# Scores with the keys on the partitions: attention of a hybrid decoder layer rewritten

## The reference

```python
# D: one shared key and value head, keys chosen by an index score
index = sum_h iw[q,h] * relu(iq[q,h] . ik[s]) * idx_scale      # causal, 8 index heads
sel = top_k(index, 256)
o_dsa = softmax(q.k[sel] * scale) . v[sel]
# nsa: two groups of four heads, three branches, gates by sigmoid
p_c = softmax(q.kc * scale)            # C: 127 compressed keys
imp = p_c summed over the 4 heads, onto 32 blocks of 64 keys by overlap
sel = top_k(imp with forced blocks, 8)
o_s = softmax over the keys of the selected blocks (S)
o_w = softmax over the last 512 keys (W)
out = g0*o_c + g1*o_s + g2*o_w
```

## Time and profile before

| | |
|---|---|
| three timed runs | 4241.75 us median (4239.13 to 4256.56) |
| profiled execution's own time, its span | 4248.7 us |
| busy in the span: PE, DVE, ACT, POOL | 3741.8, 2353.1, 1908.3, 564.5 us |
| attention, in the profile | 569 to 2475 us |
| busy there: PE, DVE, ACT, POOL | 1614, 1567, 1357, 369 us |
| granted PE clock there | 0.87 |

### The profile page before, as it was taken

How to read it: one execution, slowest core, us unless ns; L and a number is a source line. 1 busy time by engine, 2 the same in 40 slices (tenths; PEclk the granted TensorE clock), 3 DMA queues, 4 the chain that set the end, 5 groups by cost and what they waited for, 6 DMA issues and landing times. The chain is left out here.

```text
span 4248.7 us, 62435 instructions
## 1 busy us (share of the span) xinstructions
PE 3741.8 (88%) x20968; PEld 3259.9 (77%) x20968; DVE 2353.1 (55%) x6486; ACT 1908.3 (45%) x3882; POOL 564.5 (13%) x659
## 2 busy tenths in 40 slices
PE   6999677788889877977978969699999999999997
PEld 5999566677778777867877958588788878878885
DVE  4222148889888888888887534333343334324323
ACT  2000147777778766866866633232223223222221
POOL 0000022222221122122021113200020002002001
PEclk9999757888889888988988989899999999999998
DMA  4222231100000000000000035433333433333342
GB/s 144 63 63 69 63 90 34 45 27 27 27 27 27 17 11 27 17 11 21 11 11 16 4 117 158 148 94 97 126 100 98 143 104 94 111 131 99 99 133 75
DMA packets 296102, 295.35 MB, mean 70 GB/s; under 512 B 20272, under 2 KB 237616, under 8 KB 293680
## 3 DMA queue, kind: packets, MB, share of 16 engines
q1 hardware_dynamic: 294368, 290.10, 22.4%
q10 hardware_dynamic: 1488, 2.20, 0.2%
HBM read 223.58 MB, written 51.90 MB: 65 GB/s over the span
## 5 line engine op out<-in xcount | busy, mean ns | idle before, releaser
L1977 DVE TENSOR_TENSOR f_w_lo<-f_raw,f_w_hi 128x1024 fp32r<-128x1024 f32 x264 | 337.4, 1279 | 879.9 <-ACT f_w_hi L1929 879.9
L1008 PE MATMUL a_ps_t<-a_const,a_scores 128*128 128x128 f32 x2864 | 528.8, 293 | 168.9 <-ACT a_scores L1069 155.4
L1929 ACT ACTIVATE f_w_hi<-f_raw 128x1024 fp32r<-128x1024 f32 x264 | 279.9, 1060 | 878.8 <-PE f_acc L1881 327.4
L1096 ACT ACTIVATE a_p_t<-a_ps_t 128x512 f32<-128x512 f32 (+3 forms) x992 | 467.8, 480 | 207.4 <-PE a_ps_t L1008 203.1
L1069 ACT ACTIVATE a_scores<-a_scores,a_nmax 128x128 f32<-128x128 f32 (+15 forms) x512 | 457.1, 893 | 213.7 <-DVE a_nmax L1141 145.3
L1008 PEld LDWEIGHTS a_ps_t<-a_const,a_scores 128*128 128x128 f32 x2864 | 374.9, 162 | 218.3 <-ACT a_scores L1069 197.9
L1079 ACT ACTIVATE a_atleast<-a_index,a_tk 128x192 bf16<-128x192 f32 (+13 forms) x336 | 284.7, 847 | 62.1 <-DVE a_tk L1187 60.0
L974 PEld LDWEIGHTS a_ps_o<-a_vsl,a_p_t 128*128 128x128 f32 x2176 | 291.4, 196 | 15.8
L1881 PE MATMUL f_gate<-f_x_hi,f_w_hi 128*128 128x512 f32 x704 | 275.1, 391 | 30.1 <-DVE f_w_lo L1977 30.1
L974 PEld LDWEIGHTS a_ps_o<-a_dv,a_p_t 128*128 128x128 f32 x2176 | 283.0, 193 | 11.8
L1881 PE MATMUL f_acc<-f_w_hi,f_g_hi 128*128 128x512 f32 x704 | 276.5, 393 | 17.6 <-DVE f_y L2033 12.6
(11 more groups left out here) (231 smaller groups left out, 8020.1 us busy)
## 6 DMA issues: line engine op xcount, KB each, us to landing
f_raw<-in_w_gate SPq DMA_DIRECT2D x88, 512.0 KB, 3.8
f_raw<-in_w_up SPq DMA_DIRECT2D x88, 512.0 KB, 3.8
f_raw<-in_w_down SPq DMA_DIRECT2D x88, 512.0 KB, 3.7
z_scratch<-p_z SPq DMA_DIRECT2D x16, 1120.0 KB, 5.1
a_za<-z_scratch SPq DMA_DIRECT2D x16, 608.0 KB, 4.0
pw_raw<-in_w_in SPq DMA_DIRECT2D x16, 560.0 KB, 3.7
px_raw<-in_x_t SPq DMA_DIRECT2D x16, 512.0 KB, 6.4
a_nqs<-a_nq SPq DMA_DIRECT2D x32, 256.0 KB, 3.9
```

The source lines that it names most:

```text
L1008: mm = pe.transpose(ps_t[m % 2][:, (b % 4) * P:(b % 4 + 1) * P], scores[a % 3][:, b * P:(b + 1) * P], const("ident", 0, P))
L1096: act.activation(p_t[:, j % PT_RING, 0:w], ps_t[m % 2][:, 0:w], ACT.Copy).then_inc(copied, 1)
L1929: act.activation(w_hi[:, slot], raw[:, parity], ACT.Copy).then_inc(hi_done, 1)
L1977: dve.tensor_tensor(w_lo[:, slot], raw[:, parity], w_hi[:, slot].bitcast(F32), ALU.subtract).then_inc(lo_done, 1)
```

## The change

Every piece of the attention phase after the loading of keys is ordered anew. In place of units of one head there are quads of four heads that share a key head, (kind, i, g), 128 of them, and steps: one key tile of one quad, 716 in all.

- A step's score product has the keys as weights and the queries of four heads as the 512 moving columns, so that it comes out with the keys on the partitions. ACT takes the exponential straight from PSUM to `p_t`, and this is at once the left operand of the value product. Nothing is turned.
- The row maximum must be known before. A one-pass product (`scan`: high half of the queries twice, against the keys' high and low halves) is made for each head and chunk with the queries on the partitions, in one of two banks `ps_side`; DVE adds the mask and keeps the minimum in `nmax`, and writes the rest to a junk tile.
- The maximum, and for S the selected blocks, are written into free rows of the low query half, `aug`, turned by PE (`turn_aug`), and copied by ACT to `q_1`. The second score product, `k_1` by `q_1`, brings in the low half of the queries, the maximum and the block mask. The diagonal, the window's edge, the compressed keys' mask and D's mask come by a third product, in bf16, with the identity.
- Values get a column of ones, so that the row sum comes out of the value product; C's values get 32 more columns that give the importance of the blocks.
- ACT counts the whole index row. DVE moves the threshold in two instructions, at the beginning of the next step.
- `Schedule` plans the order: each side job (maximum, index chunk, prep, turning of extra rows) has a release step, a due step and a cost, and is put where the mean rate that the due steps ask for is kept.
- The swap by DMA is gone. Queries N and D share one landing tile. Before the first step stand A, N and D of tile 0 only, and PE's work for A of tiles 1 and 2 stands in the first steps.

The core of the diff:

```diff
-BANKS_S = 4
+ST_BANKS = 3
+SIDE_BANKS = 2
+Q1_RING = 3
+SIDE_COST = {"max": 727, "cmax": 600, "idx": 680, "prep": 450, "aug": 440}
...
+    def assign(self, S):
...
+        for s in range(S):
+            total, rate = 0, 0.0
+            for r, d, _, cost, _ in todo:
+                total += cost
+                rate = max(rate, total / (max(d, s) - s + 1))
+            spent = 0.0
+            while True:
+                ready = [j for j in todo if j[0] <= s]
+                if not ready:
+                    break
+                j = ready[0]
+                if j[1] > s and spent + j[3] / 2 > rate:
+                    break
...
+            def side_bank(job):
+                r = side_no[job]
+                if r >= SIDE_BANKS:
+                    what, value = reader[r - SIDE_BANKS]
+                    pe.wait_ge(masked if what == "mask" else relu_done, value)
+                return ps_side[r % SIDE_BANKS]
...
+            def score(s):
...
+                if s >= ST_BANKS:
+                    pe.wait_ge(exp_done, s - ST_BANKS + 1)
...
+                pe.matmul(out[:, :], keys((k_t, kwn_t), kc, kind, g, i, first + j, 1), q, start=True, stop=False)
+                mm = pe.matmul(out[:, :], keys((k_1, kwn_1), kc_1, kind, g, i, first + j, 1), q_1[:, n % Q1_RING, :, :], start=False, stop=mask is None)
+                if mask is not None:
+                    mm = pe.matmul(out[:, :], mask, ident_b[:, :].unsqueeze(1).broadcast_to([P, 4, P]), start=False, stop=True)
...
+            for s in range(S + PV_LAG):
+                for job in sides[s]:
+                    side(job)
+                if s < S:
+                    score(s)
+                if s >= PV_LAG:
+                    pv(s - PV_LAG)
...
+            def turn_aug(n):
...
+                pe.wait_ge(aug_set, set_no[n] + 1)
+                bank_free(m)
+                for h in range(4):
+                    mm = pe.transpose(turn_bank(m)[:, h * P:(h + 1) * P], aug[q_kind(kind)][:, 4 * g + h, :], const("ident", 0, P))
+                mm.then_inc(group_turned, 1)
+                pe.wait_ge(group_turned, m + 1)
```

ACT's order, and DVE's:

```diff
+            for s in range(S):
+                for job in sides[s]:
...
+                exps(s)
+                for t, m in plan.counts[s]:
+                    count(t, m)
...
+            waiting = []
+            for s in range(S + PV_LAG):
+                while waiting:
+                    move_threshold(*waiting.pop(0))
+                for job in sides[s]:
...
+                if s in finish_at:
+                    finish(finish_at[s])
```

More of the change, by code:

```diff
@@ L476 @@
 CONST_COLS = _at
[L479 to L489, removed]
+KEPT_COLS = CCOL["win"]
+PREP_BLOCKS = {"A": ((0, 3), (3, 3), (6, 4), (10, 4)), "N": ((0, 4), (4, 4)), "D": ((0, 4), (4, 4))}
+PREP_EVACS = {"A": (2, 3, 1, 1), "N": (1, 1), "D": (1, 1)}
 def key_tiles(kind, i):
@@ L498, in key_tiles @@
     return 0, i + 1
-def attention_phase(nc, z, consts, kc, vc, o_mix):
[L503 to L550, removed]
-    n_evac = 0
[L553 to L587, removed]
@@ L682, in attention_phase, with staged @@
         o_tiles = o_mix.rearrange("(t p) n -> t p n", p=P)
-        quad = {n: a_of[n] // 4 for n in att}
-        def wait_reader(eng, s):
-            if s >= BANKS_S:
-                kind, value = reader[s - BANKS_S]
-                eng.wait_ge(masked if kind == "mask" else relu_done, value)
-        def qk_before(n):
-            return chunk0[n + 1]
+        stage = index[1]
+        def staged(name, rows=slice(0, P), lo=0, n=None):
+            c = CCOL[name] - KEPT_COLS + lo
+            return stage[rows, c:c + (dict(CONST)[name] if n is None else n)]
@@ new lines, in prep_iq @@
+            def prep_iq(t):
+                iqx = part("iq", 8, IDX_DIM).unsqueeze(2).broadcast_to([P, 8, 2, IDX_DIM])
+                iqs = split[:, 6:14, :].rearrange("p h (a d) -> p h a d", a=4)
+                last = mine(pool.tensor_copy(iqs[:, :, 0:2, :], iqx))
+                pool.wait_ge(own, last)
+                last = mine(pool.tensor_tensor(iqs[:, :, 2:4, :], iqx, iqs[:, :, 0:2, :].bitcast(F32), ALU.subtract))
+                pool.wait_ge(own, last)
+                pool.sem_inc(split_done["A"], 1)
@@ new lines, in side @@
+            def side(job):
+                if job[0] == "max":
+                    scan(job)
+                elif job[0] == "idx":
+                    index_part(job)
+                elif job[0] == "prep":
+                    prep(job)
+                else:
+                    turn_aug(job[1])
+            pe.wait_ge(const_ld, 32)
+            for job in first_prep:
+                prep(job)
+            pe.wait_ge(rows_set, 1)
+            for s in range(S + PV_LAG):
[5 more added lines that the diff above has]
+                    pv(s - PV_LAG)
@@ new lines, in _ @@
+            for m in (1, 2, 0):
+                key_rows(m)
+            waiting = []
+            for s in range(S + PV_LAG):
+                while waiting:
+                    move_threshold(*waiting.pop(0))
+                for job in sides[s]:
+                    if job[0] == "max":
+                        mask(job)
+                        if job == last_max[job[1]]:
+                            set_aug(job[1])
+                    elif job[0] == "idx":
+                        index_unit(job)
+                    elif job[0] == "prep" and job[1] == "A" and job[3] == 3:
+                        gates(job[2])
+                if s in finish_at:
+                    finish(finish_at[s])
+                if s >= S:
+                    continue
+                i = quads[steps[s][0]][1]
+                off = s - plan.tile0[i]
+                if off == 0 and i >= 2:
+                    above_mask(i)
+                if off == 1 and 1 <= i < TILES - 1:
+                    set_search(i + 1)
+                if s == plan.kept_at.get(i):
+                    kept_mask(i)
+                for m, c in enumerate(plan.counts[s]):
+                    if m + 1 < len(plan.counts[s]):
+                        move_threshold(*c)
+                    else:
+                        waiting.append(c)
```

1021 lines of the change are left out of this document (555 added, 466 removed).

## The result

The changed kernel takes 4638.51 us (median of 4, 4621.84 to 4647.35) against 4245.01 for the kernel before (4239.13 to 4256.56): a ratio of 1.0919 [1.0892, 1.0945]. It is 9% slower, where 3% faster was forecast, and it lies outside the range.

What follows compares the result with a forecast made beforehand. DVE was taken as tightest before; afterwards the count chain from tile 5. Attention's end, 578 + 221 + 1321 + 150 = 2270, plus 90 of clock gives 2360 for 2475: 4127 us, forecast 4060 to 4200, full range 3900 to 4330.

Steps and rivals of the forecast that it cites:

- the same share and so the same clock: Attention: PE busy for 83% as now, so clock stays 0.87 to 0.90, costing 147 us, 90 on the path.
- only 60% of it counts: Attention: of the 147 us that the low clock costs PE, about 60% is on the path, 90 us.
- The chain: Attention, from tile 5: exponential, count, threshold, maxima, scan, score take 3.5 + 0.83 w/1000 us per two steps; tiles 5 to 14, 1321.
- near 1.5: Last tiles: DVE waits for ACT's count before the threshold row, near 1.5 us each.
- PE and 24 rounds of about 1.3 us: Tiles 1 to 4: PE and 24 count rounds set the time, 41, 50, 59, 71 us, together 221.
- Sums of work: Attention: PE 1475 us at full clock, DVE 1193, ACT about 1110.
- Rival 1: Attention: the chain doesn't bind, PE goes through and ends at 2076 us; kernel 3843 us; chance 0.13.
- Rival 2: Attention: removing transposes brings the clock to 1.0, so the 90 us are not lost; kernel 4037 us; chance 0.10.
- Rival 3: Tiles 5 to 14: count rounds longer than reckoned, 1.0 us more each makes 4367 us; chance 0.23 (4265 and up).
- Tile 14 not shorter than 163: Sign of the forecast: tile 14, 163 us before the change, gets no shorter.
- Tiles 1 to 5 some 15 us shorter: Sign of the forecast: tiles 1 to 5 each get some 15 us shorter.

Runs made afterwards that it cites:

- run 6: Changed kernel with the 336 counts and threshold moves left out, three side banks and two score banks: 4267.09 us.
- run 16: Changed kernel with threshold moved behind side jobs, three side banks, and turnings without PE's own wait and one step later: 4264.47 us, ratio 1.0037.
- run 14: Changed kernel with threshold moved behind side jobs, three side banks, and PE not waiting for its own turnings' end, their place unchanged: 4301.24 us.
- run 2: Changed kernel with DVE's threshold move placed behind the step's side jobs, not ahead of them: 4486.69 us.
- run 3: Changed kernel with three side banks in place of two, and two score banks in place of three: 4465.86 us.
- run 7: Changed kernel with counts made on ACT but not read by DVE; threshold stays at -1e20, every key kept: 4413.09 us.
- run 9: First product of each score left out, on the changed kernel with late threshold move and three side banks (4382.56 us): 4514.08 us.
- run 11: Scans and maxima cut to 128 keys per chunk, on the changed kernel with late threshold move and three side banks (4382.56 us): 4763.52 us.
- run 12: Maxima cut to 128 keys per chunk, scans full, on the changed kernel with late threshold move and three side banks (4382.56 us): 4370.54 us.
- run 4: Changed kernel with a 512-column bf16 product of zeros added between the two score products of each of 716 steps: 4659.72 us.

## Why the prediction was wrong

- **The failed step is the clock**: "I expect the same share and so the same clock". PE's share was indeed the same, 83% (85% before), and the clock fell to 0.80. The prediction gave the clock 147 us of PE's time, 90 of them on the path; PE's busy time at half speed was 764 us, which costs 382. The 147 were near what the kernel before pays (163), so it is the step from the share to the clock that failed, and not its price at the same clock. That only 60% of it counts was taken from no row. The prediction had named PE's idle pieces as what brings the clock down, and did not ask what its own new waits would do.
- **How the miss divides.** The forecast's length of attention was 2360 - 569 = 1791 us: 1475 of work, 147 of low clock, and 169 left as idle time of PE. Measured: 1511, 382 and 400, together 2293. So the miss of 502 us is 235 of clock, 231 of idle time and 36 of busy time reckoned at full clock. The two large parts are not independent, since the edits that took waits away brought the clock up with them.
- **The chain** was right as a chain, and mis-sized. DVE waited 415.4 us for counts, 260 times, 1.6 us each ("near 1.5"); PE's scans waited 176.3 us for maxima. Tiles 5 to 14 took 1633 us for 1321; run 6, without counts and with a third bank, took 1389, and run 16, with counts, 1340. Two things were missing in its sum: PE at half speed lengthens the chain's own PE parts, and the waits for the ends of turnings, counted as 0.3 us of PE's work each for 128 of them (38 us), cost 81 us by run 14.
- **Tiles 0 to 4.** Tile 0 was to end at 578; tile 1's first selection came at 668. Tiles 1 to 4 took 423 us for 221. From 600 to 965 PE has a clock of 0.67 and is idle for 27% of the time. Even run 16 needs 360 for tiles 1 to 4. "PE and 24 rounds of about 1.3 us" left out what a quad of few steps has to wait for: scan, maximum, set, turning, copy. How this splits into chain and clock was not tested, so the cause of the slow start stays open.
- **Sums of work** held: PE between 1451 us (run 16) and 1511 (the changed kernel) at full clock (1475 forecast), DVE 1209 us (1193 forecast), ACT 1136 (1110), ACT's exponential 601 ns (600). PE's step with mask at full clock takes 1.60 us by starts in tile 15; the terms make it 0.84 + 0.55 + 0.23 = 1.62. The mask product costs 0.23 (2833.57 to 2833.80), as taken. Tile 15, forecast as PE alone at 150, took 138.
- **Rival 1** fell: it put attention at 1507 us (2076 - 569), and even without counts it took 1981.
- **Rival 2** fell, on the wrong side. The transposes of exponentials went, and the clock fell from 0.87 to 0.80. By the rule of the Trainium skill ("TensorE: Matmul & The Clock Gate", Part 4, PE-mode transpose) that transposes don't count as activity, products in their place should have held the clock up; the rows don't bear that out here. With nearly the idle time of the kernel before (278 us, 292 before) run 16 has a clock of 0.88 for 0.87: it stands about where it stood with the 2864 transposes of exponentials. Too much else differs between the two for a clean test of the rule.
- **Rival 3** had the sign, the place and the mechanism, and a price (4367) that lacked the clock. Runs 2, 3, 7 and 14 show its parts: the place of the wait, the banks, the wait for counts, the turnings. I gave it 0.23; the chance of a fall of the clock, as the price that any new wait of PE can bring, stood nowhere.
- "Tile 14 not shorter than 163" held (214). "Tiles 1 to 5 some 15 us shorter" did not.

## What to carry to other kernels

Cost a new wait of TensorE not by its length alone but with the half speed that can follow it: here, with 122 us of idle time, 255 us of busy time went too, for the same instructions. Put waits for results behind the work that feeds TensorE, and let TensorE signal without waiting for itself. Taking wide products away can make a kernel slower (runs 9 and 11), so read the granted clock of each stage before trimming its work.

## What the runs showed that was not expected

- TensorE was busy for 112.09 of 114 us at a granted clock of 0.50 (run 11), and in tile 14 of the changed kernel for 49.55 of 50 us at 0.50. The Trainium skill, "TensorE: Matmul & The Clock Gate", Why this matters for your kernels, advises to keep TensorE busy to get the full clock; these rows show busy stretches that don't get it. More than half of a step in run 11 are value products (eight of 65 columns, one load of weights each: by the starts 1.56 of 2.78 us).
- Less work made the kernel slower twice (131 and 381 us), and 716 products more cost 21 us in the changed kernel. Which property of a product holds the clock up stays open: runs 11 and 12 differ in the width of the scans, run 9 leaves out products and run 4 adds some, and no run holds all but one property of the products fixed.
